# Stick-breaking attention: the rounding of the softplus moved from VectorE to GpSimd

## The reference

```
z = einsum('bqhd,bkhd->bhqk', qb, kb) * scale
log_fail = where(mask, log_sigmoid(-z), 0.0)
after = cumsum(log_fail, axis=3, reverse=True) - log_fail
log_a = log_sigmoid(z) + after
a = where(mask, exp(log_a), 0.0)
out = einsum('bhqk,bkhd->bqhd', a, vb)
```

## Time and profile before

| | |
|---|---|
| median of 3 runs | 3323.29 us (3318.3 to 3324.28) |
| the profiled execution | 3321.17 us |
| its span, first to last instruction | 3319.4 us |
| the stage of the change | 214.5 to 396.5 us, 182.0 us |
| DVE busy between 222 and 388 us | 160.70 of 166.00 us |
| ACT, PE busy there | 147.36 us, 158.75 us |
| POOL busy there | 0 |

### The profile page before, as it was taken

How to read it: one execution, slowest core, us unless ns; L and a number is a source line. 1 busy time by engine, 2 the same in 40 slices (tenths; PEclk the granted TensorE clock), 3 DMA queues, 4 the chain that set the end, 5 groups by cost and what they waited for, 6 DMA issues and landing times. The chain is left out here.

```text
span 3319.4 us, 34592 instructions
## 1 busy us (share of the span) xinstructions
PE 3051.0 (92%) x13364; PEld 2400.0 (72%) x13364; DVE 1566.3 (47%) x1477; ACT 784.0 (24%) x1000; POOL 1040.8 (31%) x476
## 2 busy tenths in 40 slices
PE   6999897999999996879999796799888999999997
PEld 5876474888888884768888564676676788888885
DVE  3649927455545556451120566545434443333335
ACT  2148813111111115120021234133202211111111
POOL 2320032343443442323343311300233434334341
PEclk9999998999999998989999698779899999999998
DMA  2121020222222221121123330200231111111111
GB/s 102 50 57 26 1 95 26 77 88 88 88 82 88 79 86 51 32 92 48 51 95 107 84 77 26 63 13 14 102 121 38 45 51 47 48 51 44 51 51 57
DMA packets 64786, 206.82 MB, mean 62 GB/s; under 512 B 8512, under 2 KB 14912, under 8 KB 63808
## 3 DMA queue, kind: packets, MB, share of 16 engines
q1 hardware_dynamic: 61024, 191.56, 18.2%
q10 hardware_dynamic: 3680, 14.16, 1.1%
HBM read 165.77 MB, written 17.83 MB: 55 GB/s over the span
## 5 line engine op out<-in xcount | busy, mean ns | idle before, releaser
L232 POOL TENSOR_TENSOR w_hi<-w_raw,inv_count 128x1024 fp32r<-128x1024 f32 x203 | 388.0, 1911 | 1877.3 <-PE ps L257 1259.7
L235 POOL TENSOR_TENSOR w_lo<-w_raw,w_hi 128x1024 fp32r<-128x1024 f32 x203 | 523.3, 2578 | 15.9
L257 PE MATMUL ps<-x_hi,w_hi 128*128 128x512 f32 x1344 | 418.0, 392 | 24.0 <-POOL w_lo L235 9.9
L257 PE MATMUL ps<-x_hi,w_lo 128*128 128x512 f32 x1344 | 417.2, 392 | 0.0
L257 PE MATMUL ps<-x_lo,w_hi 128*128 128x512 f32 x1344 | 416.7, 391 | 0.0
L257 PEld LDWEIGHTS ps<-x_hi,w_hi 128*128 128x128 f32 x1344 | 254.5, 190 | 79.0 <-issue 16.0
L257 PEld LDWEIGHTS ps<-x_lo,w_hi 128*128 128x128 f32 x1344 | 254.4, 189 | 53.3
L257 PEld LDWEIGHTS ps<-x_hi,w_lo 128*128 128x128 f32 x1344 | 254.2, 189 | 53.3
L257 PE MATMUL ps<-hidden_lo,w_hi 128*128 128x512 f32 x864 | 266.0, 389 | 0.0
L257 PE MATMUL ps<-hidden_hi,w_lo 128*128 128x512 f32 x864 | 266.0, 389 | 0.0
L257 PE MATMUL ps<-hidden_hi,w_hi 128*128 128x512 f32 x864 | 266.0, 389 | 0.0
(11 more groups left out here) (335 smaller groups left out, 4522.0 us busy)
## 6 DMA issues: line engine op xcount, KB each, us to landing
w_raw<-wall SPq DMA_DIRECT2D x221, 512.0 KB, 3.6
ada_raw<-wada SPq DMA_DIRECT2D x48, 512.0 KB, 4.2
gates_scratch<-gate_out ACTq DMA_DIRECT2D x16, 512.0 KB, 2.7
residual<-x_t SPq DMA_DIRECT2D x8, 512.0 KB, 8.5
residual<-x_t SPq DMA_DIRECT2D x2, 2048.0 KB, 9.8
residual_scratch<-residual SPq DMA_DIRECT2D x1, 4096.0 KB, 12.2
fox_k_both<-fox_split_k SPq DMA_DIRECT2D x32, 128.0 KB, 2.3
fox_q_both<-fox_split_q SPq DMA_DIRECT2D x32, 128.0 KB, 2.3
```

The costliest lines, as they stand in the source:

```text
L232: nc.gpsimd.tensor_tensor(w_hi[:, slot, :], w_raw[:, slot, :], one.to_broadcast([P, S]), ALU.mult).then_inc(w_split, 1)
L235: nc.gpsimd.tensor_tensor(w_lo[:, slot, :], w_raw[:, slot, :], w_hi[:, slot, :].bitcast(F32), ALU.subtract).then_inc(w_split, 1)
L257: last = nc.tensor.matmul(ps[:, banks + c, :], lhs, x[:, k0 + k, c * HALF:(c + 1) * HALF], start=(left == nk * 3 - 1), stop=(left == 0))
```

## The change

`high` is taken out of DVE's loop and given to POOL, as a `tensor_scalar` that multiplies by 1.0 twice, for each of the 80 blocks behind the wait for that block's softplus. `low` stays on DVE and stands at the head of the loop's turn, as `low(i + 1)`, ahead of `add_later(i)`. The wait that guards the ring of four buffers against PE's reads is now made twice, by POOL for `sph` and by DVE for `spl`.

```diff
@@ gpsimd
                 nc.gpsimd.memset(t[:, :, :, :].bitcast(F32), 0.0).then_inc(q_zeroed.sem, 1)
+            pool.wait_ge(*q_zeroed.at(2))
+            for k in range(NS):
+                pool.wait_ge(*sp_done.at(k + 1))
+                pool.wait_ge(*sph_done.at(k))
+                if k >= 4:
+                    if last_of_chunk(k - 4):
+                        pool.wait_ge(*c_full.at(k - 3))
+                    else:
+                        pool.wait_ge(*t_done.at(sums_to(k - 4)))
+                nc.gpsimd.tensor_scalar(at(sph, k), at(sp_buf, k), 1.0, 1.0, ALU.mult, ALU.mult
+                                        ).then_inc(sph_done.sem, 1)
@@ vector
-            def high(k):
-                dve.wait_ge(*sp_done.at(k + 1))
+            def low(k):
                 if k >= 4:
                     if last_of_chunk(k - 4):
                         dve.wait_ge(*c_full.at(k - 3))
                     else:
                         dve.wait_ge(*t_done.at(sums_to(k - 4)))
-                nc.vector.tensor_copy(at(sph, k), at(sp_buf, k)).then_inc(sph_done.sem, 1)
-
-            def low(k):
                 dve.wait_ge(*sph_done.at(k + 1))
                 nc.vector.tensor_tensor(at(spl, k), at(sp_buf, k), at(sph, k).bitcast(F32), ALU.subtract
                                         ).then_inc(spl_done.sem, 1)
@@ vector
             for i in range(-2, NS + 3):
+                if 0 <= i + 1 < NS:
+                    low(i + 1)
                 if 0 <= i < NS:
                     add_later(i)
                 if 0 <= i + 2 < NS:
                     softplus(i + 2)
-                    high(i + 2)
-                    low(i + 2)
                 if i >= 3 and last_of_chunk(i - 3):
                     output(i - 3)
```

## The result

| | before | changed |
|---|---|---|
| median | 3323.43 us (6 runs, 3318.3 to 3324.5) | 3344.53 us (6 runs, 3335.12 to 3346.75) |
| ratio | | 1.0066, 95% interval 1.0052 to 1.008 |
| span of the profiled execution | 3319.4 us | 3339.4 us |
| first softplus to last output copy | 178.84 us | 197.37 us |

The change costs 21 us; 3342 was forecast. The ratio's interval is 17 to 27 us above the kernel before: a loss that is clear of the noise, and under 1% of the whole. Of the 20.0 us by which the two profiled spans differ, 18.5 lie in the stage (the last row of the table, from the starts of the two instructions). What comes after the stage is 1.8 us longer in this execution, and that is the runs' own spread: in the thirteen profiled kernels of this study, which differ in this stage alone, it took between 2921.0 and 2931.2 us (2923.8 before, 2925.6 with the change).

The account below looks back on a forecast made before the run. DVE was taken to bound the stage; +26.0 us for the longer way from softplus to `low`, less 5.0 for hidden output copies, gave +21.0 us on 3321.2, so 3342 us, range 3329 to 3362.

Parts of the forecast that it names:

- The bound: Stage between two barriers: DVE sets the pace, so changes to its row of starts move the end one for one.
- No slack for the round trip: DVE's order: `low` right behind its block's softplus, nothing can run ahead, so each block pays the whole POOL round trip.
- DVE to POOL: Handover from the end of DVE's softplus to the start of POOL's copy: 0.07 us.
- POOL's instruction: POOL's copy, estimated from its 128x1024 row and two MEMSETs: 0.62 us full block, 0.41 us half.
- the rival of a POOL slow on small tiles: POOL's copy takes twice DVE's CAST, 0.86 and 0.58 us: +39 us, 3360; chance 0.10.
- POOL to DVE: Handover from the end of POOL's copy to the start of DVE's `low`: 0.14 us.
- Softplus to low: DVE, start to start: 1.17 to 1.51 us full, 0.77 to 1.03 half; +26.0 us over all blocks.
- Hidden copies: 15 output copies now stand between softplus and `low`, covered by DVE's wait: -5.0 us.
- Sum: Profiled execution: +26.0 - 5.0 = +21.0 us, from 3321.2 to 3342.2 us.
- Contention: `low`, with two SBUF inputs, never runs beside POOL's copy; the output copy reads PSUM, so no slowdown.
- Not slower: Rival: round trip as short as what it replaces, POOL's instruction 0.34 us or less: 3321 us; chance 0.05.
- The clock: Rival: TensorE's clock falls to 1.2 GHz as PE waits longer: +64 us on top, about 3400; chance 0.02.

Follow-up runs that it names:

- POOL short: Changed kernel, but from block 12 on POOL copies only 16 columns of each head, all waits kept: 3315.89 us, ratio 0.9983.
- POOL twice: Changed kernel with the same POOL copy made into a spare tile ahead of each copy: 3383.58 us, ratio 1.0189.
- The run with the copies behind `low`: Kernel before with POOL making the high part, DVE's turn otherwise as before, output copies not moved: 3347.54 us, ratio 1.0078.
- the run with `add_later` in between: Changed kernel with DVE's turn reordered to softplus(i+2), add_later(i), low(i+1): 3415.84 us, ratio 1.0282.
- a deeper pipeline with one more exchange on ACT: Changed kernel, softplus, scores, exp and log one block earlier, four softplus buffers, ACT making probability(i-1) ahead of log(i+3): 3312.74 us; with five `a_buf` buffers 3308.66.
- the two runs with softplus first: Changed kernel with softplus(i+2) heading DVE's turn: followed by low(i+1), add_later(i), 3363.06 us; followed by add_later(i), low(i+1), 3415.84 us.
- the run one block deeper: Changed kernel with scores, exp, log and softplus one block earlier and four softplus buffers: 3321.71 us, ratio 1.0005.
- the run with both waits taken away: Changed kernel one block deeper, plus probability(i-1) ahead of log(i+3) on ACT and five `a_buf` buffers: 3308.66 us, ratio 0.9962.
- the last control: Kernel before with the one block deeper pipeline, probability first on ACT and five `a_buf` buffers, CAST kept on DVE: 3315.24 us, ratio 0.9981.

## Why the prediction was right

Step by step, with what was measured:

- **The bound.** Right: DVE's row set the stage. Each change to that row came out in the stage one for one, in both directions (POOL short, POOL twice). It holds down to a stage of 173 us and with the order of the change; in the runs with a shorter row still, other waits came up.
- **No slack for the round trip.** Right, and the step on which all hung: the order shows that `low(k)` stood directly behind `softplus(k)` before and after. The one wait of the stage that grew on DVE is that of `low`, 53.9 us over 76 blocks put down to POOL and the 3.2 of the other four, 57.1 in all, for about 57 forecast (62 less the copies; its own terms, 64 x 0.83 + 16 x 0.62, give 63 and not 62).
- **DVE to POOL** 0.07 us, measured 0.08. **POOL's instruction** 0.62 and 0.41, measured 0.621 and 0.406. The step from the 128x1024 row and the two MEMSETs was good, and the rival of a POOL slow on small tiles is out. **POOL to DVE** 0.14, measured 0.10 on the mean of the full blocks (0.11 in the step shown): taken from a wait of PE, and DVE is a little quicker.
- **Softplus to low.** 1.51 and 1.03, measured 1.48 and 1.00 to 1.01; the first half block has 1.84, for 1.50 before, since POOL's two MEMSETs came first. Before, the CAST itself took 1.00 us beside them, as the prediction had it. The sum was 26.0, and measured are 64 x 0.31 + 4.1 = 23.9 us. This is the only term that was mis-sized, by 2 us; the handover to DVE, 0.04 us shorter in each of 80 blocks, is most of it.
- **Hidden copies.** -5.0, and the row with the copy shows it: 1.48 us with or without. The run with the copies behind `low` gives 5.9 in the stage.
- **Sum.** 23.9 - 5.0 = 18.9, and the stage is 18.5 longer. The medians say 21, and the interval of the ratio is 17 to 27 us, so that the +21.0 forecast met the median as closely as it did is luck by some 2 us.
- **Contention.** Right for this change: `low` 693 ns as before. The runs with `low` beside POOL show what was avoided, and that it falls on whichever of the two starts second: on POOL's copy in most blocks, 1.00 us for 0.62, and on `low` in some, 0.99 for 0.69.
- **Not slower.** The turning point was put at a POOL instruction of 0.34 us. At 0.22 the run was 3 to 8 us faster than before by its interval, which fits, and the stages put the point at about 0.31.
- **The clock.** It stayed at 1.00, with PE waiting more. That the rival was a real one shows in the run with `add_later` in between, where PE waits longer still and the clock falls.
- **What the prediction did not see.** It said that a real gain would need `low` behind the next `add_later`, and left it there. With `low` behind the next softplus the wait for POOL does go, and the kernel still got slower; of the orders tried, only a deeper pipeline with one more exchange on ACT gave a gain, 12.7 us in the stage and not 34.7, and 5.1 of these need no POOL. The order that the prediction named, softplus(k), add_later(k - 1), low(k), softplus(k + 1), was not tried: the two runs with softplus first both put `low(k)` behind softplus(k + 1) too. It keeps the loop of three blocks. In the kernel before, PE's sums end 1.48 us behind the start of `low` (301.40 to 302.88, the latter the end of PE's matmul of 302.48), and `add_later` could start 1.21 us behind it, so DVE would stand some 0.27 us; by the starts of the earlier trace rows the step would be 0.61 + 0.60 + 0.27 + 0.60, about 2.1 us for 2.39. That is an estimate which no run shows.

## What to carry to other kernels

Work moved from the bounding engine to an idle one costs the whole round trip, both handovers included, when the very next instruction of the bounding engine needs the result; look at the order on each engine, not at where a call stands in the text, and price the round trip from rows. To hide it, other work of the same engine has to stand in between, and then every loop through the engines has to be counted again, in blocks per turn: a wait that goes is replaced by that of the loop with the next longest time per block. Where an engine's row is the bound, an instruction that need not wait for the one right before it is cheaper than one that must.

## What the runs showed of the hardware

- One-input `tensor_scalar` on POOL, f32 to fp32r, 128 partitions: 0.218 us at 32 elements, 0.406 at 256, 0.621 at 512, and 1.05 at 1024; a straight line of 0.19 us and 0.84 ns an element.
- POOL's copy and `low`, with two inputs in SBUF, side by side: the one that starts second does its work per element only when the first has ended. With `low` 0.17 us ahead, as in the first pair below, from the run one block deeper, the copy takes 1.00 us and ends 0.48 us behind `low`; a copy of 256 elements ends 0.26 us behind it. The difference, 0.22 us for 256 elements, is the 0.84 ns an element of the copy alone, and what passes beside `low` is 0.14 us of the 0.19 that do not depend on the size. With POOL 0.17 us ahead, as in the second pair, from the run with both waits taken away, POOL keeps its 0.62 us and `low` takes 0.99 for 0.69. The means in that run, 0.86 us for the copy of a full block and 0.74 for `low`, are mixtures of these cases. The Trainium skill (SBUF — State Buffer, "Who interferes with whom") calls the port pair that the two engines share an exclusive lock; the trace agrees, with the 0.48 and 0.26 us.

```profile
299.76 0.68 DVE L825 TENSOR_TENSOR stick_sp_lo<-stick_sp,stick_sp_hi 128x512 fp32r<-128x512 f32 x1
299.93 0.99 POOL L768 TENSOR_SCALAR stick_sp_hi<-stick_sp 128x512 fp32r<-128x512 f32 x1 [1.10 <-DVE stick_sp L814]
...
235.54 0.62 POOL L768 TENSOR_SCALAR stick_sp_hi<-stick_sp 128x512 fp32r<-128x512 f32 x1 [0.94 <-DVE stick_sp L814]
235.71 0.99 DVE L825 TENSOR_TENSOR stick_sp_lo<-stick_sp,stick_sp_hi 128x512 fp32r<-128x512 f32 x1
```

- DVE's handover to itself is not free: 0.71 us from the start of a full softplus to a CAST that reads its result (the kernel before), 0.60 to one that does not (the last control).
